# Hybrid decoder layer on one core: the recurrence's outputs and half of its keys transposed by VectorE and scratch memory

## The chip, the cores and the metric

The kernel runs on one core of a Trainium2 chip. The metric is the device time of one execution in microseconds.

## What is computed

One layer of a decoder with two branches. A prompt of 2048 rows of 1024 numbers is normalised and modulated (h) and projected by one weight. Branch A is sliding-window attention over 128 rows with sinks. Branch B is a gated linear recurrence with four heads of 128: with decay f, keys k, queries q and values i, each head carries a 128x128 state over the rows. Both branches are gated with a SiLU, projected, merged by sigmoid gates and projected back.

```
o, s_new = hgrn2_chunked(q, log_f, k_in, i, s0)
yb = rms_norm(o, o_norm_g) * silu(zb)
g_a, g_b = split(sigmoid(h @ w_merge + b_merge))
y = g_a * (ya @ w_proj_a) + g_b * (yb @ w_proj_b)
out = x + gate * (y @ w_out)
```

Beside the prompt, eight sample rows go through the same layer with their own caches and states. Everything is fp32.

## The kernel before, in words

The prompt is worked off in 4 blocks (`it`) of 512 rows, each of 4 tiles of 128. A block is a list of 68 dense units (`UNITS`, line 36): 4 "B" and 4 "A" (attention's projections), 4 each of "za", "f", "qb", "ib", "zb" (units 8 to 27), then from unit 28 the merges: "ga" and "gb" (sigmoid gates, units 28 to 35 are 0 to 3 of both), "pa" and "pb" (the branches' projections, from unit 36 and 37 on), and from unit 60 the output. A dense unit is 24 matmuls with a moving tile of 512 ("pa" and "pb": 12), since every operand is split into a high and a low part of a reduced format and three products are added. Units alternate between the PSUM banks D0 and D1.

Everything else of TensorE is a side task, hung behind one half of a dense unit: `at_half(it, n, ...)` puts a task behind half n, so half 70 is the first half of unit 35 and half 71 the second. All engines walk through the same list of units and halves in order, each doing its part of a task; the numbers in the list are the whole schedule. In a second half the order is fixed: ScalarE first evacuates the unit (`evac`; for a gate it waits for the unit's end), then makes the high parts of the weight blocks attached to it (`split_hi`), and then the side tasks; GpSimd first makes the low parts of those weight blocks (`split_lo`, four subtractions), then the side tasks.

The recurrence in a block, with all of it transposed so that the head's 128 features lie on the partitions:

- seven levels (halves 42 to 54) build the decayed `qq`, `kk` and the score matrix `AT`;
- for tile t at unit 28 + t: "KT" turns the keys of the tile, [features, rows] to [rows, features], with four TensorE transposes into bank XC, and ScalarE copies them to `kst` (lines 936 and 1125); in the second half "o" makes the output rows (into XB; ScalarE copies it into `kk` in place of the keys and squares it into `acc` for the norm), and "st" makes the state update with `kst` as weights (into XA; VectorE adds it to `state`);
- "onorm" (unit 32): VectorE computes the four tiles' root mean squares and scales the outputs in `kk`;
- "yT" (halves 67 to 70, a tile each): TensorE turns the scaled outputs back to [features, rows] with four transposes, VectorE multiplies them with the gate `szb` into a slot of `yf`, ScalarE makes the high part `yb_hi` (`high`), GpSimd the low part `yb_lo` (`low`, line 1713).

The first "pb" (unit 37, half 74) waits until all four low parts are there: `s.wait_ge("yl", 16 * it + 8)` (line 735).

SyncE issues all DMAs from one queue, in order. A weight block of 512 KB (`w_raw`, a ring of three) is loaded when the block three before it has been split (`weights`, line 528). Other transfers are events in the same queue, placed by unit (`later`, line 539). In blocks 0 and 1 "bursts" on TensorE (line 797) multiply the raw weight blocks with the sample's rows, and wait for their loads.

Of the kernel before, what the change touches and what calls it, by code (L numbers as in the profile page):

```python
# [15 lines left out]
TB, NIT = 512, 4  # L16
P, KT, NT = 128, D // 128, TB // 128
# [114 lines left out]

AHEAD = {0: (), 1: (5, 7), 2: (1, 3, 5, 7), 3: (1, 3, 5, 7)}
# [23 lines left out]
for it in range(NIT):  # L157
# [38 lines left out]
    for _t in range(NT):  # L196
        put(it, 28 + _t, 0, "KT", _t, "XC")
        put(it, 28 + _t, 1, "o", _t, "XB")
        put(it, 28 + _t, 1, "st", _t, "XA")
    put(it, 32, 0, "onorm", 0)  # L200
    for _t in range(NT):
        at_half(it, 67 + _t, "yT", _t, "XB" if _t % 2 else "XA")
# [47 lines left out]
for _it in range(NIT):  # L250
    for _u in UNITS:
        if _u in TH:
# [6 lines left out]
           "lvl", "dgp", "at0", "smax", "p_exp", "p_norm", "kst", "on", "yf", "yh", "yl", "y7f", "y7h", "y7l", "x_in0", "x_in1", "xst", "rstd",  # L259
# [63 lines left out]
def build(nc, A, O):  # L323

    ctx = ExitStack()
    with ctx:
# [53 lines left out]
        acc = sb("acc_t", [P, TB])  # L380
        kst = sb("kst_t", [P, HB, P])
# [11 lines left out]
        AT32 = kst[:, :, :].rearrange("p h (t i) -> p (h t) i", t=NT)  # L393
# [12 lines left out]
        first.close()  # L406
        yb_hi, yb_lo = sb("yb_hi_t", [P, 4, TB], F32R), sb("yb_lo_t", [P, 4, TB], F32R)
# [6 lines left out]
        szb = qT  # L414
        y_hi, y_lo = sb("y_hi_t", [P, KT, TB], F32R), sb("y_lo_t", [P, KT, TB], F32R)
# [87 lines left out]
        def _(sp):  # L503
# [36 lines left out]
            for it in range(NIT):  # L540
# [6 lines left out]
                later.setdefault(b0 + 5, []).append(("vr", it, 0))  # L547
                later.setdefault(b0 + 59, []).append(("xr", it, 0))
# [14 lines left out]
            def event(what, it, a):  # L563
                if what == "xst":
# [108 lines left out]
        def _(pe):  # L673
# [88 lines left out]
            def side(it, task, a, key):  # L762
# [209 lines left out]
        def _(act):  # L972
# [99 lines left out]
            def side(it, task, a, key):  # L1072
# [52 lines left out]
                elif task == "KT":  # L1125
                    s.full(*key)
                    if it or a:
                        s.full(*((it, "st", a - 1) if a else (it - 1, "st", 3)))
                    s.free(fn(kst[:, :, :], bank[:, :].rearrange("p (h n) -> p h n", h=HB), ACT.Copy), *key)
                elif task == "o":  # L1130
                    s.full(*key)
                    if it or a:
                        s.freed(*((it, "o", a - 1) if a else (it - 1, "o", 3)))
                    fn(kk[:, :, P * a:P * a + P], bank[:, 0:512].rearrange("p (h n) -> p h n", h=HB), ACT.Copy)
                    for h in range(HB):
                        ins = fn(acc[:, P * h:P * h + P], bank[:, P * h:P * h + P], ACT.Square,
# [9 lines left out]
            for it in range(NIT):  # L1146
                for u in range(NU):
                    for hf_ in (0, 1):
# [9 lines left out]
                        for task, a, _, key in SIDE.get((it, u, hf_), []):  # L1158
# [10 lines left out]
                            if task == "yT":  # L1169
                                s.freed(it, "yT", a)  # L1170
# [8 lines left out]
        def _(dve):  # L1179
# [244 lines left out]
            def side(it, task, a, key):  # L1424
# [117 lines left out]
                elif task == "st":  # L1542
# [4 lines left out]
                    free(ins, *key)  # L1547
                elif task == "onorm":
                    s.freed(it, "o", 3)
                    do(ts(oss, oss, 1.0 / P, EPS, ALU.mult, ALU.add))  # L1550
                    rsqrt(orst, oss, ow1, ow2)
                    for t in range(NT):
                        o = kk[:, :, P * t:P * t + P]
                        s.done(tt(o, o, orst[:, HB * t:HB * t + HB].unsqueeze(2).broadcast_to([P, HB, P]), ALU.mult), "on")
# [294 lines left out]
```

## Time and profile before

| what | us |
|---|---|
| median of three runs (1558.32 to 1558.43) | 1558.33 |
| span of the profiled execution | 1555.9 |
| TensorE busy | 1527.1 |
| GpSimd busy | 826.0 |
| VectorE busy | 787.0 |
| ScalarE busy | 540.7 |

For the profiled execution the span, from its first to its last instruction, is what is listed; its own device time is not listed beside it. The page gives busy times, the span in slices, and the chain of work that ended last, followed back from the last instruction to what released it at each step. TensorE's rows are pipelined: one row's duration is longer than the distance to the next, so distances between starts tell what a stretch costs. The mean granted clock over the span is 0.996.

### The profile page before, as it was taken

To read this page: it belongs to the slowest core of one execution; us is meant where nothing else is said; L and a number is where in the kernel's file an instruction comes from. 1 tells how busy PE (TensorE), PEld (TensorE's weight loads), DVE (VectorE), ACT (ScalarE), POOL (GpSimd) and SP (SyncE) were. 2 spreads that over 40 slices of the span, in tenths; PEclk is the share of its full clock that TensorE was granted. 3 is DMA by queue.
4 is the path that set the end of the run, shared out by engine and by line. 5 is a ranking of instruction groups with operands and counts; after the bars stand their busy time and mean duration, and the time that the engine had idled before them with its cause. 6 is when DMAs were issued, how large, how long until landed. Compare 5 with 4: busy or idle time off the path is not lost.

```text
span 1555.9 us, 31655 instructions
## 1 busy us (share of the span) xinstructions
PE 1527.1 (98%) x13048; PEld 1243.0 (80%) x13048; DVE 787.0 (51%) x1900; ACT 540.7 (35%) x1119; POOL 826.0 (53%) x1074
## 2 busy tenths in 40 slices
PE   5999999999999999999999999999999999999998
PEld 2777788877888788888779878888888978888886
DVE  4767464234558866232544774622453775623132
ACT  4334324334322532434331452243432353143330
POOL 0525434557863643365773472437786363437671
PEclk9999999999999999999999999999999999999999
DMA  9612211334453321233343231223544231222351
GB/s 339 243 55 83 83 57 55 111 133 158 168 197 108 110 70 57 82 109 108 137 164 135 92 120 43 83 66 114 208 154 149 75 110 56 78 72 91 102 167 60
DMA packets 62790, 178.94 MB, mean 115 GB/s; under 512 B 7086, under 2 KB 18695, under 8 KB 61864
## 3 DMA queue, kind: packets, MB, share of 16 engines
q1 hardware_dynamic: 62648, 176.93, 33.4%
q8 instruction: 103, 1.69, 0.5%
q14 instruction: 39, 0.32, 0.1%
HBM read 162.84 MB, written 11.96 MB: 112 GB/s over the span
## 4 chain that ended last, share of the span: by engine, by line
PE 95%; DVE 3%; DMA 1%; SPq 1%; issue 1%; ACT 0%; DVEq 0%
PE ps_D L758 56%; PE ps_D L755 25%; PE ps_XCD L820 2%; PE ps_XB L896 1%; PE ps_XB L949 1%; PE ps_XA L954 1%; PE ps_XA L921 1%; PE ps_XA L932 1%; PE ps_XB L948 1%; PE ps_XA L896 1%; DMA th_t<-in_w_ada 1%; SPq L507 1%; PE ps_XB L932 0%; PE ps_XCD L831 0%; PE ps_XCD L939 0%
## 5 line engine op out<-in xcount | busy, mean ns | idle before, releaser
L1702 POOL TENSOR_TENSOR w_lo_t<-w_raw,w_hi_t 128x256 fp32r<-128x256 f32 x920 | 681.0, 775 | 599.7 <-ACT w_hi_t L980 599.4
L758 PE MATMUL ps_D<-h_hi_t,w_hi_t 128*128 128x512 f32 x1024 | 411.2, 402 | 0.0
L758 PE MATMUL ps_D<-h_hi_t,w_lo_t 128*128 128x512 f32 x1024 | 399.6, 390 | 0.0
L758 PE MATMUL ps_D<-h_lo_t,w_hi_t 128*128 128x512 f32 x1024 | 399.5, 390 | 0.0
L980 ACT ACTIVATE w_hi_t<-w_raw 128x1024 fp32r<-128x1024 f32 x232 | 240.0, 1051 | 124.6 <-PE ps_D L755 61.6
L758 PEld LDWEIGHTS ps_D<-h_hi_t,w_hi_t 128*128 128x128 f32 x1024 | 192.3, 188 | 46.3 <-issue 8.9
L758 PEld LDWEIGHTS ps_D<-h_hi_t,w_lo_t 128*128 128x128 f32 x1024 | 192.2, 188 | 41.8
L758 PEld LDWEIGHTS ps_D<-h_lo_t,w_hi_t 128*128 128x128 f32 x1024 | 192.6, 188 | 36.5
L755 PE MATMUL ps_D<-w_hi_t,h_hi_t 128*128 128x384 f32 (+1 forms) x384 | 141.6, 369 | 1.0 <-DVE yf_t L1342 1.0
L755 PE MATMUL ps_D<-w_lo_t,h_hi_t 128*128 128x384 f32 (+1 forms) x384 | 136.6, 356 | 0.0
L755 PE MATMUL ps_D<-w_hi_t,h_lo_t 128*128 128x384 f32 (+1 forms) x384 | 136.3, 355 | 0.0
L755 PE MATMUL ps_D<-w_hi_t,y_hi_t 128*128 128x512 f32 x256 | 100.2, 391 | 1.5 <-issue 1.5
L755 PE MATMUL ps_D<-w_hi_t,y_lo_t 128*128 128x512 f32 x256 | 99.6, 389 | 0.0
L755 PE MATMUL ps_D<-w_lo_t,y_hi_t 128*128 128x512 f32 x256 | 99.6, 389 | 0.0
L1376 DVE SCALAR_TENSOR_TENSOR acc_t<-th_t,ps_D 128x512 f32<-128x512 f32 x24 | 16.5, 688 | 130.8 <-PE ps_D L758 130.8
L755 PEld LDWEIGHTS ps_D<-w_hi_t,h_hi_t 128*128 128x128 f32 x384 | 72.7, 189 | 11.4 <-issue 4.9
L1047 ACT ACTIVATE th_t<-ps_D,bm_half 128x512 f32<-128x512 f32 x48 | 33.1, 690 | 139.2 <-PE ps_D L758 139.2
L1123 ACT ACTIVATE p_or_hf<-p_or_hf,sm 128x160 f32<-128x160 f32 x128 | 53.3, 419 | 68.5 <-DVE sm L1503 66.6
L755 PEld LDWEIGHTS ps_D<-w_lo_t,h_hi_t 128*128 128x128 f32 x384 | 72.6, 189 | 5.3
L755 PEld LDWEIGHTS ps_D<-w_hi_t,h_lo_t 128*128 128x128 f32 x384 | 72.8, 190 | 4.7
L1394 DVE TENSOR_TENSOR acc_t<-ps_D,gate_bc 128x512 f32<-128x512 f32 x32 | 22.1, 692 | 107.1 <-PE ps_D L755 107.0
L1456 DVE TENSOR_TENSOR qq<-qq,ff 128x1024 f32<-128x1024 f32 x28 | 40.7, 1452 | 68.6 <-PE ps_XB L896 44.7
(386 smaller groups left out, 2332.9 us busy)
## 6 DMA issues: line engine op xcount, KB each, us to landing
w_raw<-in_w_blocks SPq DMA_DIRECT2D x232, 512.0 KB, 3.4
xr<-in_x_prompt SPq DMA_DIRECT2D x16, 512.0 KB, 5.0
x_or_AT<-in_x_prompt SPq DMA_DIRECT2D x14, 512.0 KB, 4.8
out_dram<-xr SPq DMA_DIRECT2D x12, 512.0 KB, 2.8
x_or_AT<-in_x_turned SPq DMA_DIRECT2D x3, 1024.0 KB, 5.6
p_or_hf<-in_x_turned SPq DMA_DIRECT2D x3, 1024.0 KB, 6.2
out_dram<-xr SPq DMA_DIRECT2D x8, 256.0 KB, 2.0
ibtok<-vtok SPq DMA_DIRECT2D x8, 192.0 KB, 3.5
```

The lines of the kernel that those rows point to most:

```text
L507: s.done(sp.dma_start(dst, src, **kw), name, by=16)
L755: ins = mm(bank[:, 0:P * nb].rearrange("p (n c) -> p n c", c=P), a[:, k, P * j:P * j + P], w[:, s0:s0 + nb, k, :], start=go, stop=end)
L758: ins = mm(bank[:, :], w[:, s0, k0 + k, :], a[:, k, :], start=go, stop=end)
L820: ins = mm(dst, hS[:, k, :], raw[:, :, k, :], start=k < 4, stop=k >= 4)
L896: ins = mm(bank[row:row + left, m * col:m * col + m], kk[:, h, c + 32 * g:c + 32 * g + left], right, start=True, stop=True)
L980: s.done(fn(w_hi[:, SLOT[n % NB]], w_raw[:, n % NRAW], ACT.Copy), "w_hi")
L1047: s.leave(fn(dst, bank[:, :], ACT.Tanh, scale=0.5, bias=bm_half[:, c:c + 1]), it, u)
L1123: fn(p_t[:, m, :], p_t[:, m, :], ACT.Exp, bias=negm[:, m:m + 1], accum_out=rsum[:, m:m + 1])
L1376: leave(stt(acc[:, :], thx("ga", j), 1.0, bank[:, :], ALU.add, ALU.mult), it, u)
L1394: leave(tt(acc[:, 0:w], bank[:, 0:w], gate_bc[:, c0:c0 + w], ALU.mult), it, u)
L1456: s.done(tt(qr, qr, fl[:, :, :, 0:1].broadcast_to(shape), ALU.mult))
L1702: ins = g_.tensor_tensor(w_lo[:, c, k:k + 2], w_raw[:, n % NRAW, k:k + 2], f32(w_hi[:, c, k:k + 2]), ALU.subtract)
```

## The change

Two kinds of TensorE turns are replaced: all of "yT" (16 turns in all), and "KT" for tiles 2 and 3 (8 turns). In their place VectorE transposes a half of `kk` (two tiles, 4 x 256 columns) in place, in blocks of 32x32; SyncE stores the half to scratch memory (`zk`, `zo`, 512 KB), waits until it has landed, and loads it back with four DMAs whose pieces are runs of 32 numbers, so that the blocks come to stand where a full transpose has them. Each half has its own store and loads: "ks" and "kl" for the keys, "os" and "ol" for the two halves of the output.

- The keys' half (`kD`, half 56) lands in `k_turned`, and "st" 2 and 3 read it as weights there. ScalarE's "o" 2 waits for the keys' store before it overwrites them.
- The norm is done in two halves (halves 60 and 64), each ending with the transpose (`oD`).
- "yD" (halves 65, 66, 69, 70) is VectorE's multiplication with the gate, out of the loaded half; "yT" (halves 66, 67, 70, 71) is now only the high part on ScalarE and the low part on GpSimd.
- The loaded outputs lie over `acc` and `kst`, and over `qq`; ScalarE's squares go to a slot of `yf` instead of `acc`.

```diff
+KEYS_TURNED = (1,)
+O_AT, ON_AT, YD_AT, YT_AT = (57, 59, 61, 63), (60, 64), (65, 66, 69, 70), (66, 67, 70, 71)
+KS_AT, KL_AT, OS_AT, OL_AT = (28, 28), (28, 28), (30, 32), (31, 32)
...
     for _t in range(NT):
-        put(it, 28 + _t, 0, "KT", _t, "XC")
-        put(it, 28 + _t, 1, "o", _t, "XB")
-        put(it, 28 + _t, 1, "st", _t, "XA")
-    put(it, 32, 0, "onorm", 0)
+        if _t // 2 not in KEYS_TURNED:
+            put(it, 28 + _t, 0, "KT", _t, "XC")
+        at_half(it, O_AT[_t], "o", _t, "XB")
+        at_half(it, O_AT[_t], "st", _t, "XA")
+    for _r in KEYS_TURNED:
+        at_half(it, 56, "kD", _r)
+    for _r in range(2):
+        at_half(it, ON_AT[_r], "onorm", _r)
     for _t in range(NT):
-        at_half(it, 67 + _t, "yT", _t, "XB" if _t % 2 else "XA")
+        at_half(it, YD_AT[_t], "yD", _t)
+        at_half(it, YT_AT[_t], "yT", _t)
...
+                if what == "ks":
+                    s.wait_ge("kD", len(KEYS_TURNED) * it + KEYS_TURNED.index(a) + 1)
+                    s.wait_ge(f"kt_in{a}", 64 * it)
+                    load(zk[a].rearrange("i q (h t) j p -> (i q) h (t j p)", t=2), kk[:, :, half], f"kz{a}")
+                elif what == "kl":
+                    s.wait_ge(f"kz{a}", 16 * (it + 1))
+                    for j in range(4):
+                        load(k_turned[32 * j:32 * j + 32, a].rearrange("p h t (i c) -> p (h t) i c", c=32),
+                             zk[a, :, :, :, j].rearrange("i q n p -> q n i p"), f"kt_in{a}")
+                elif what == "os":
+                    s.wait_ge("oD", 2 * it + a + 1)
+                    s.wait_ge(f"ot_in{a}", 64 * it)
+                    load(zo[a].rearrange("i q (h t) j p -> (i q) h (t j p)", t=2), kk[:, :, half], f"oz{a}")
+                elif what == "ol":
+                    s.wait_ge(f"oz{a}", 16 * (it + 1))
+                    s.full(it, "o" if a else "st", 3 if a else 1)
+                    for j in range(4):
+                        load(o_turned[a][32 * j:32 * j + 32].rearrange("p h t (i c) -> p (h t) i c", c=32),
+                             zo[a, :, :, :, j].rearrange("i q n p -> q n i p"), f"ot_in{a}")
...
                 elif task == "st":
-                    s.freed(it, "KT", a)
+                    if a < 2:
+                        s.freed(it, "KT", a)
+                    else:
+                        s.wait_ge("kt_in1", 64 * (it + 1))
                     for h in range(HB):
-                        ins = mm(bank[:, P * h:P * h + P], kst[:, h, :], ibtok[:, a, P * h:P * h + P],
+                        left = kst[:, h, :] if a < 2 else k_turned[:, 1, h, a % 2, :]
+                        ins = mm(bank[:, P * h:P * h + P], left, ibtok[:, a, P * h:P * h + P],
                                  start=True, stop=True)
-                elif task == "yT":
-                    s.wait_ge("on", 4 * it + a + 1)
-                    for h in range(HB):
-                        ins = tr(bank[:, P * h:P * h + P], kk[:, h, P * a:P * a + P], ident[:, :])
...
+                elif task == "kD":
+                    half = kk[:, :, 256 * a:256 * a + 256]
+                    do(v.transpose(half, half), "kD")
                 elif task == "onorm":
-                    s.freed(it, "o", 3)
-                    do(ts(oss, oss, 1.0 / P, EPS, ALU.mult, ALU.add))
-                    rsqrt(orst, oss, ow1, ow2)
-                    for t in range(NT):
+                    s.freed(it, "o", 2 * a + 1)
+                    c, half = slice(8 * a, 8 * a + 8), kk[:, :, 256 * a:256 * a + 256]
+                    do(ts(oss[:, c], oss[:, c], 1.0 / P, EPS, ALU.mult, ALU.add))
+                    rsqrt(orst[:, c], oss[:, c], ow1[:, c], ow2[:, c])
+                    for t in (2 * a, 2 * a + 1):
...
+                    s.settle()
+                    do(v.transpose(half, half), "oD")
-                elif task == "yT":
-                    s.full(*key)
-                    free(stt(yf_slot(16 * it + 4 + a), bank[:, 0:512].rearrange("p (h n) -> p h n", h=HB), og_half[:, 0:1],
-                             szb[:, :, P * a:P * a + P], ALU.mult, ALU.mult), *key)
+                elif task == "yD":
+                    s.wait_ge(f"ot_in{a // 2}", 64 * (it + 1))
+                    do(stt(yf_slot(16 * it + 4 + a), o_turned[a // 2][:, :, a % 2], og_half[:, 0:1],
+                           szb[:, :, P * a:P * a + P], ALU.mult, ALU.mult), "yt")
```

GpSimd's list in block 0, from the recurrence to the merges, before: `yb_lo_t` is the low part of y, `w_lo_t<-w_raw` the splits of weight blocks (four rows a block).

```order
L1702 TENSOR_TENSOR w_lo_t<-w_raw,w_hi_t 128x256 x52
L1718 TENSOR_TENSOR yb_lo_t<-yf_t,yb_hi_t 128x4x128 x2
L1702 TENSOR_TENSOR w_lo_t<-w_raw,w_hi_t 128x256 x4
L1718 TENSOR_TENSOR yb_lo_t<-yf_t,yb_hi_t 128x4x128 x2
L1702 TENSOR_TENSOR w_lo_t<-w_raw,w_hi_t 128x256 x8
```

And now:

```order
L1753 TENSOR_TENSOR w_lo_t<-w_raw,w_hi_t 128x256 x48
L1769 TENSOR_TENSOR yb_lo_t<-yf_t,yb_hi_t 128x4x128
L1753 TENSOR_TENSOR w_lo_t<-w_raw,w_hi_t 128x256 x4
L1769 TENSOR_TENSOR yb_lo_t<-yf_t,yb_hi_t 128x4x128
L1753 TENSOR_TENSOR w_lo_t<-w_raw,w_hi_t 128x256 x4
L1769 TENSOR_TENSOR yb_lo_t<-yf_t,yb_hi_t 128x4x128
L1753 TENSOR_TENSOR w_lo_t<-w_raw,w_hi_t 128x256 x4
L1769 TENSOR_TENSOR yb_lo_t<-yf_t,yb_hi_t 128x4x128
```

The four low parts stood in two pairs, both ahead of the split attached to unit 35. Now they stand singly, a split before each of the last three; the last low part is behind unit 35's split. It is the same in the other blocks.

SyncE's queue in block 0, from the weight loads of the levels to the load of x for the next block's norm, before:

```order
L507 DMA w_raw<-in_w_blocks 128x1024 x26
L507 DMA x_or_AT<-in_x_prompt 128x1024 x2
L507 DMA w_raw<-in_w_blocks 128x1024 x5
```

And now (`z_k`, `z_o` are the scratch memory):

```order
L522 DMA w_raw<-in_w_blocks 128x1024 x22
L522 DMA z_k<-kk 512x1x256
L522 DMA k_turned<-z_k 32x32x32 x4
L522 DMA w_raw<-in_w_blocks 128x1024 x2
L522 DMA z_o<-kk 512x1x256
L522 DMA acc_or_kst<-z_o 32x32x32 x4
L522 DMA w_raw<-in_w_blocks 128x1024 x2
L522 DMA z_o<-kk 512x1x256
L522 DMA qq<-z_o 32x32x32 x4
L522 DMA x_or_AT<-in_x_prompt 128x1024 x2
L522 DMA w_raw<-in_w_blocks 128x1024 x5
```

Three stores with four loads each now stand among the weight loads (in blocks 1 to 3 one weight load stands between the first output store and its loads). Since otherwise loads follow their store at once, the queue waits at each for the store to land.

## Rows read from the trace of the kernel before

**Rows 1.** The page: span, TensorE busy, and the engines on the chain that ended last.

```profile
span 1555.9 us, 31655 instructions
...
PE 1527.1 (98%) x13048; PEld 1243.0 (80%) x13048; DVE 787.0 (51%) x1900; ACT 540.7 (35%) x1119; POOL 826.0 (53%) x1074
...
PE 95%; DVE 3%; DMA 1%; SPq 1%; issue 1%; ACT 0%; DVEq 0%
```

**Rows 2.** Timeline of TensorE, block 2: first matmuls of half 67, "pa" 0, "pb" 0 (start us, us, instruction).

```profile
1045.50 0.39 PE L758 MATMUL ps_D<-h_hi_t,w_hi_t 128*128 128x512 f32 x1
...
1061.09 0.39 PE L758 MATMUL ps_D<-w_hi_t 128*128 128x512 f32 x1
...
1063.81 0.39 PE L758 MATMUL ps_D<-yb_hi_t,w_hi_t 128*128 128x512 f32 x1
```

**Rows 3.** Timeline of TensorE, block 2: first matmuls of both halves of units 30 and 32.

```profile
1019.99 0.48 PE L758 MATMUL ps_D<-h_hi_t,w_hi_t 128*128 128x512 f32 x1
...
1023.16 0.48 PE L758 MATMUL ps_D<-h_hi_t,w_hi_t 128*128 128x512 f32 x1
...
1037.24 0.48 PE L758 MATMUL ps_D<-h_hi_t,w_hi_t 128*128 128x512 f32 x1
...
1040.06 0.39 PE L758 MATMUL ps_D<-h_hi_t,w_hi_t 128*128 128x512 f32 x1
```

**Rows 4.** Timeline of TensorE, block 0: the sample's turn beside unit 30.

```profile
263.62 0.66 PE L831 MATMUL ps_XCD<-ident,srow 128*128 128x128 f32 x4 [0.69 <-ACT kst_t L1129]
```

**Rows 5.** VectorE: a block transpose (ns, min/median/max), and block 2's norm in the timeline.

```profile
L1527 DVE STREAM_TRANSPOSE p_or_hf<-p_or_hf x32: 845/845/848, 110.7 to 1299.2; 128x640 f32<-128x640 f32 x32
...
1037.59 1.12 DVE L1545 SCALAR_TENSOR_TENSOR state<-state,ff,ps_XA 128x128 f32<-128x128 f32 x4 [7.50 <-PE ps_XA L954]
1038.75 0.65 DVE L1550 TENSOR_SCALAR sm<-sm 128x16 f32<-128x16 f32 x1
...
1042.36 2.50 DVE L1554 TENSOR_TENSOR kk<-kk,sm 128x512 f32<-128x512 f32 x4
```

**Rows 6.** The DMA view of 452 to 461 us, and a DMA issue of the page.

```profile
DMA packets 4377, 2.84 MB, mean 315 GB/s; under 512 B 140, under 2 KB 4195, under 8 KB 4375
...
out_dram<-xr SPq DMA_DIRECT2D x12, 512.0 KB, 2.8
```

**Rows 7.** Timeline of ScalarE, block 2, around the start of "pa" 0.

```profile
1059.34 0.63 ACT L1069 ACTIVATE yb_hi_t<-yf_t 128x512 fp32r<-128x512 f32 x1 [2.34 <-DVE yf_t L1557]
1061.29 0.69 ACT L1047 ACTIVATE th_t<-ps_D,bm_half 128x512 f32<-128x512 f32 x1 [1.31 <-PE ps_D L758]
1061.87 2.00 ACT L980 ACTIVATE w_hi_t<-w_raw 128x1024 fp32r<-128x1024 f32 x2
```

**Rows 8.** Timeline of GpSimd, block 2, the same stretch.

```profile
1056.57 2.82 POOL L1702 TENSOR_TENSOR w_lo_t<-w_raw,w_hi_t 128x256 fp32r<-128x256 f32 x4 [1.12 <-ACT w_hi_t L980]
1059.36 2.54 POOL L1718 TENSOR_TENSOR yb_lo_t<-yf_t,yb_hi_t 128x512 fp32r<-128x512 f32 x2
1063.00 6.06 POOL L1702 TENSOR_TENSOR w_lo_t<-w_raw,w_hi_t 128x256 fp32r<-128x256 f32 x8 [1.11 <-ACT w_hi_t L980]
```

**Rows 9.** Timeline of TensorE, block 1: first matmuls of "pa" 0 and "pb" 0.

```profile
687.88 0.39 PE L758 MATMUL ps_D<-w_hi_t 128*128 128x512 f32 x1
...
691.79 0.40 PE L758 MATMUL ps_D<-yb_hi_t,w_hi_t 128*128 128x512 f32 x1
```

**Rows 10.** Timeline of VectorE, block 0: the state update of tile 3.

```profile
279.59 1.12 DVE L1545 SCALAR_TENSOR_TENSOR state<-state,ff,ps_XA 128x128 f32<-128x128 f32 x4 [8.65 <-PE ps_XA L954]
```

**Rows 11.** Timeline of SyncE's queue, block 0: three weight loads, the first at 288.77.

```profile
288.77 8.13 SPq L507 DMA_DIRECT2D w_raw<-in_w_blocks  x3
```

**Rows 12.** Windows before unit 0: us, busy us of each engine (instructions), PEclk, DMA share, GB/s.

```profile
28.50:32.00 3.50, 3.50 (x18) 0.85 (x12) 3.02 (x10) 0.97 (x2) 1.03 (x1) 0.53 1.06 414
35.00:38.50 3.50, 1.95 (x16) 1.86 (x16) 3.47 (x6) 2.48 (x4) 0.73 (x3) 1.00 0.65 220
38.50:45.50 7.00, 5.34 (x20) 5.34 (x21) 6.29 (x19) 2.33 (x4) 5.90 (x7) 0.51 1.00 408
```

More of the change, by code:

```diff
@@ L379, in build @@
         qa, q3 = (yf[:, :, c:c + w].rearrange("p s (n d) -> p s n d", d=DH) for c, w in ((0, 384), (384, 128)))
-        acc = sb("acc_t", [P, TB])
-        kst = sb("kst_t", [P, HB, P])
+        acc_kst = sb("acc_or_kst", [P, 2 * TB])
+        acc, kst = acc_kst[:, 0:TB], acc_kst[:, TB:].rearrange("p (h n) -> p h n", h=HB)
         hS, yS = sb("hS_or_yS", [P, KT, 32]), sb("cT_or_ab", [P, KT, 32])
@@ L392, in build @@
         ps_s = kst[0:8]
-        AT32 = kst[:, :, :].rearrange("p h (t i) -> p (h t) i", t=NT)
+        AT32 = kst.rearrange("p h (t i) -> p (h t) i", t=NT)
         sq_in = ibS[:, 0:256]
@@ L406, in build @@
         first.close()
+        k_turned = first.enter_context(nc.sbuf_tensor("k_turned", [P, 2, HB, 2, P], F32))
+        first.close()
+        first = ExitStack()
         yb_hi, yb_lo = sb("yb_hi_t", [P, 4, TB], F32R), sb("yb_lo_t", [P, 4, TB], F32R)
@@ L414, in build @@
         szb = qT
+        o_turned = [t.rearrange("p (h t n) -> p h t n", h=HB, t=2)
+                    for t in (acc_kst[:, :], qq.rearrange("p h n -> p (h n)")[:, 0:1024])]
+        zk, zo = (nc.dram_tensor(f"z_{n}", [2, 4, 32, 2 * HB, 4, 32], F32).ap() for n in "ko")
         y_hi, y_lo = sb("y_hi_t", [P, KT, TB], F32R), sb("y_lo_t", [P, KT, TB], F32R)
@@ L547, in _ @@
                 later.setdefault(b0 + 5, []).append(("vr", it, 0))
+                for r in range(2):
+                    if r in KEYS_TURNED:
+                        later.setdefault(b0 + KS_AT[r], []).append(("ks", it, r))
+                        later.setdefault(b0 + KL_AT[r], []).append(("kl", it, r))
+                    later.setdefault(b0 + OS_AT[r], []).append(("os", it, r))
+                    later.setdefault(b0 + OL_AT[r], []).append(("ol", it, r))
                 later.setdefault(b0 + 59, []).append(("xr", it, 0))
@@ L563, in event @@
             def event(what, it, a):
-                if what == "xst":
+                half = slice(256 * a, 256 * a + 256)
+                if what == "ks":
[17 more added lines that the diff above has]
+                             zo[a, :, :, :, j].rearrange("i q n p -> q n i p"), f"ot_in{a}")
+                elif what == "xst":
                     s.full(it, "o", 3)
@@ L1126, in side @@
                     s.full(*key)
-                    if it or a:
-                        s.full(*((it, "st", a - 1) if a else (it - 1, "st", 3)))
-                    s.free(fn(kst[:, :, :], bank[:, :].rearrange("p (h n) -> p h n", h=HB), ACT.Copy), *key)
+                    if a:
+                        s.full(it, "st", a - 1)
+                    s.free(fn(kst, bank[:, :].rearrange("p (h n) -> p h n", h=HB), ACT.Copy), *key)
                 elif task == "o":
@@ L1133, in side @@
                         s.freed(*((it, "o", a - 1) if a else (it - 1, "o", 3)))
+                    if a // 2 in KEYS_TURNED:
+                        s.wait_ge(f"kz{a // 2}", 16 * (it + 1))
+                    s.wait_ge("yl", 16 * it + 4)
                     fn(kk[:, :, P * a:P * a + P], bank[:, 0:512].rearrange("p (h n) -> p h n", h=HB), ACT.Copy)
                     for h in range(HB):
-                        ins = fn(acc[:, P * h:P * h + P], bank[:, P * h:P * h + P], ACT.Square,
+                        ins = fn(yf[:, 1, P * h:P * h + P], bank[:, P * h:P * h + P], ACT.Square,
                                  accum_out=oss[:, HB * a + h:HB * a + h + 1])
@@ L1169, in _ @@
                             if task == "yT":
-                                s.freed(it, "yT", a)
+                                s.full(it, "st", 3)
+                                s.wait_ge("yt", 4 * it + a + 1)
                                 high(yb_hi[:, :, P * a:P * a + P], 16 * it + 4 + a)
```

4 lines of the change are left out of this document (2 added, 2 removed).

## Prediction

> **What bounds the kernel now.** I read the page first [rows 1]: TensorE is busy for 1527.1 of 1555.9 us and has 95% of the chain that ended last. So a microsecond that another engine saves is worth nothing unless TensorE waits for it, one taken from TensorE's list is worth itself, and one that TensorE has to wait comes on top. The sum is made on this span, 1555.9 us. The median of the three runs, 1558.3 us, is 2.4 us longer; I carry this difference over unchanged. About 0.2% (3.1 us) is what a measurement of this kernel can tell from no change.
>
> The second view is TensorE's timeline around the turns. A half unit of the dense work takes 2.72 us when nothing stands in it (the first matmul of "pa" 0 to that of "pb" 0) [rows 2]. From half 67 to "pa" 0 there are five halves with four turns of y in them: 1061.09 - 1045.50 = 15.59 us where five bare halves are 13.60 [rows 2]. A turn of y (four transposes, and the dense matmuls refilling behind them) therefore costs 0.50 us, though its four records add up to 1.1. A turn of the keys costs what unit 30's first half has over unit 32's, which also follows "o" and "st" but holds nothing: 3.17 against 2.82 us, plus some 0.13 us of refilling in the next half: 0.48 us [rows 3].
>
> **What comes off TensorE.** 16 turns of y at 0.50 are 8.0 us, and 8 turns of the keys (tiles 2 and 3 of each block) at 0.48 are 3.8 us. One stall goes as well: in block 0 the sample's turn at unit 30 waited 0.69 us for ScalarE's copy of the turned keys out of the bank that both use [rows 4]; that copy is gone. **Sum: 12.5 us less**, some 3 us of it in each block, and all of it on the path.
>
> **What is added and hidden.** VectorE gets three block transposes of 1024 elements a block, and the 14 small steps of the norm twice instead of once. A transpose of 640 elements takes 0.845 us, so one of 1024 is about 1.35 us; the norm's small steps run from 1038.75 to 1042.36, 3.6 us [rows 5]. That is some 8 us a block on an engine that is 51% busy, beside dense work on TensorE. I cost it at nothing by itself; it matters where a transfer starts behind it.
>
> No row of before has pieces of 128 bytes in bulk. The nearest is the load of the sample states: in 9 us the engines moved 4195 packets under 2 KB, almost all of 512 bytes, at 315 GB/s [rows 6]. 4096 pieces of 512 bytes (2.1 MB) at that rate take 6.7 us. A set of four loads has 4096 pieces of 128 bytes: by bytes alone 1.7 us, by pieces 6.7 us, and twice that, 13.3 us, if a short piece costs double. I take 6.7 us, because the count of pieces is the same, and add 1.5 us for issue and landing. The store moves 512 KB like the stores of the output, 2.8 us to landing [rows 6].
>
> The keys have slack: turned at the start of unit 28, they are wanted at the end of unit 30, three units on. With SyncE coming to the store some 6 us late (it first waits for a split of weights), store and loads end about 17 us after the start of unit 28; "st" 2 is due after some 25 us.
>
> The second half of the output has less. In block 2 VectorE ends "st" 3 at 1038.7, now 1.0 us earlier; norm 3.6, two scalings 1.25 (half of the 2.50), the transpose 1.35, store 2.8, loads 8.2: it lands at about 1055.0. "pa" 0 will start at 1061.1 - 3.0 = 1058.1. So yD 2 and 3 are done in time for what follows, with some 2 us to spare.
>
> **What is added and not hidden** is the place of the last piece of y. It was handed over at half 70 and is now at half 71, and at a second half ScalarE and GpSimd do other things first. ScalarE takes the gate of unit 35 out of the bank, which it can't before that unit ends, then copies the high part of a weight block, and only then the high part of y; GpSimd splits that weight block before it makes the low part. The trace has this chain without the y: with "pa" 0 starting at 1061.09, ScalarE's gate starts at 1061.29, the weight copy at 1061.87 [rows 7], GpSimd's split at 1063.00 [rows 8]. A split is 2.82 us, the low part of a y tile half of 2.54, so the low part of tile 3 is ready 1.91 + 2.82 + 1.27 = 6.0 us after "pa" 0 starts. "pb" 0, whose first matmul waits for all of it, would start after 2.7 us [rows 2]. **TensorE stalls 3.3 us** in a block like 2 or 3. In block 1 a burst stands in the way and "pb" 0 starts 3.9 us after "pa" 0 [rows 9]: 2.1 us. These stalls don't depend on how fast the transfers are.
>
> In block 0 two more things are late. There VectorE has "st" 3 done at 280.7 [rows 10], 1.7 us earlier now; by the same steps the loads are issued at about 288 and done at 296. Only then come the two x tiles and the weight block that SyncE issued at 288.77 before [rows 11]; 1.5 MB at 315 GB/s is 5 us, so that block lands at 301. ScalarE wants it at about 297 and holds its queue, the y tiles among it. Worked through, the low part of tile 3 comes 2.9 us later than above: 6.2 us. If the pieces go at the byte rate this part is zero, and both ends are kept.
>
> Stalls: 6.2 + 2.1 + 3.3 + 3.3 = 14.9 us. The clock adds something. Before unit 0, after a stretch with only 16 matmuls of nine columns in 3.5 us, the granted clock fell from 1.00 (2.4 GHz) to about 0.5 (1.2 GHz): 0.53 over 3.5 us once, 0.51 over 7 us once [rows 12]. Dense work that runs 3.5 us at half rate loses 1.7 us. A stall of 3.3 us is shorter than what came before those falls, one of 6.2 is not: from none to four falls, and I take two, 3.4 us. By the Trainium skill, page TensorE: Matmul & The Clock Gate (Rules for kernel authors), gaps between matmul bursts put the array back on the lower clock; if that held for all four stalls, the sum would be 3.4 us longer than mine.
>
> **The sum:** 1555.9 - 12.5 + 14.9 + 3.4 = 1561.7 us of span, 5.8 us more, or a time of **1564.1 us**, 0.4% slower.
>
> **Rival 1: the short pieces are slow.** If a 128-byte piece costs twice a 512-byte one, a set takes 6.7 us longer. In blocks 2 and 3 it then lands 4.7 us after yD 2 is wanted, in block 1 about 4, in block 0 the full 6.7 counts, and four falls of the clock are likely: 14.9 + 20 + 6.8 - 12.5 = 29 us more, 1587 us. For it: each piece is a quarter of the nearest one's size, and the reads jump. Against it: 6.7 us already pays as much for a piece as for one four times as long. The Trainium skill speaks against this change here: DMA: Bandwidth & Descriptors (Rules for kernel authors) puts a plain DMA with a rearranged access pattern at 19 times the hardware's own transpose, and its Specifications say that transfers under 512 bytes run below line rate. No row shows such a factor; the pieces here are whole runs of 32 numbers. Nineteen times 1.7 us would be a set of 32 us, 19 us more in each block than this rival and some 1660 us: chance 0.02 of this rival's 0.18.
>
> **Rival 2: stalls and savings cancel.** The stall at "pb" 0 stays, but block 0 has no more than the others and the clock never falls: 3.3 x 3 + 2.1 = 12.0 against 12.5 us, 1557.8 us. This is the other side, not slower: it decides where stalls and clock together stay under 15.6 us, that is at 3.9 us a block. For it: nothing in the trace says that a stall of 3.3 us is enough for a fall, and by bytes the loads are quick. Chance 0.23.
>
> **Rival 3: faster.** If the handover of tile 3 is not what ends last, because "pb" 0's matmuls already issued hide part of the wait or the turns cost TensorE nearer 0.65 us than 0.50, the time goes down: halved stalls with no fall of the clock are 6 - 12.5, 1551.8 us. Rows 7 and 8 leave little room for this, since every step of the chain stands there with its start. Chance 0.07.
>
> **Rival 4: SyncE's queue.** SyncE now sits on the store until it has landed, and the weight loads are behind it. In blocks 0 and 1 bursts on TensorE wait for raw weights directly; in block 0 the weight block for the burst at unit 33 lands, by my steps, about a microsecond before it is wanted. If it misses, 1 to 5 us more, 1567 us. It is inside the range, at 0.10.
>
> **Chances.** Forecast 0.42, rival 1 0.18, rival 2 0.23, rival 3 0.07, rival 4 0.10. Slower by over 0.2% is the forecast, rivals 1 and 4: 0.70. Within 0.2% is rival 2: 0.23; faster 0.07. The range runs from 1557 (rival 2 with its uncertainty) to 1582 (short pieces at about 1.7 times); left out are rival 3 and the upper part of rival 1. The likeliest case has 1561 to 1570 for itself, since block 0 and the clock can each go by 3 us.
>
> **What would show it.** In the profile after: no matmuls of the y turns, and half of the key turns; a wait of TensorE for GpSimd's low part of y, four times, the first matmul of "pb" 0 behind it, 3.3 us in blocks 2 and 3 and less in block 1; dense halves at 2.72 us between them; a granted clock under 1 after some of these waits. The loads of the turned output landing some 7 to 9 us after issue show the middle price; 3 us or 14 us show its ends. The forecast is wrong if TensorE's waits at "pb" 0 sum to under 9 us, or if it waits at "st" 2 or for VectorE, which I cost at nothing.

## The result, and the profile after

| | median us | lowest to highest | against before (95%) |
|---|---|---|---|
| before, same chip | 1558.32 | 1558.03 to 1558.43 | |
| with the change | 1564.40 | 1563.17 to 1566.84 | 1.0044 (1.0030 to 1.0058) |

The change costs 6.1 us, 0.4%; 1564.1 was predicted. The profiled execution is the slowest of those after: its own time is 1566.84, its span 1564.7, 8.8 us over the span before. The page, against [rows 1]:

```profile
span 1564.7 us, 31594 instructions
...
PE 1521.3 (97%) x12952; PEld 1236.9 (79%) x12952; DVE 813.1 (52%) x1972; ACT 535.5 (34%) x1111; POOL 829.1 (53%) x1074
...
DMA packets 119048, 191.52 MB, mean 122 GB/s; under 512 B 57199, under 2 KB 74952, under 8 KB 118121
...
q8 instruction: 102, 1.67, 0.5%
...
PE 91%; DVE 4%; SPq 1%; POOL 1%; ACT 1%; issue 1%; DMA 1%; DVEq 0%
```

TensorE has 96 matmuls less and is busy 5.8 us less, and yet the span is longer: its share of the chain fell from 95 to 91%, and VectorE, GpSimd and ScalarE took most of the rest. What they hold up stands in the list of TensorE's waits (us in total, times, longest); the two of its rows that name another engine and that before did not have:

```profile
PE ps_D L799 <- POOL yb_lo_t L1769: 11.6, 4, 3.2
...
PE ps_XB L989 <- ACT yf_t L1180: 1.3, 1, 1.3
```

TensorE's timeline has the four waits, each in front of the first matmul of "pb" 0, blocks 0 to 3:

```profile
308.20 0.77 PE L799 MATMUL ps_D<-yb_hi_t,w_hi_t 128*128 128x512 f32 x1 [3.19 <-POOL yb_lo_t L1769]
...
697.42 0.48 PE L799 MATMUL ps_D<-yb_hi_t,w_hi_t 128*128 128x512 f32 x1 [2.01 <-POOL yb_lo_t L1769]
...
1068.73 0.76 PE L799 MATMUL ps_D<-yb_hi_t,w_hi_t 128*128 128x512 f32 x1 [3.19 <-POOL yb_lo_t L1769]
...
1429.34 0.47 PE L799 MATMUL ps_D<-yb_hi_t,w_hi_t 128*128 128x512 f32 x1 [3.19 <-POOL yb_lo_t L1769]
```

In block 2, where the turns of y stood in [rows 2], TensorE now runs from half 67 to "pa" 0 without a gap:

```profile
1049.06 0.39 PE L799 MATMUL ps_D<-h_hi_t,w_hi_t 128*128 128x512 f32 x1
...
1062.66 0.39 PE L799 MATMUL ps_D<-w_hi_t 128*128 128x512 f32 x1
```

The five halves take 13.60 us, as bare as they can be, where it was 15.59. And this is the chain behind the wait, ScalarE's and GpSimd's timelines against [rows 7, 8]:

```profile
1062.86 0.69 ACT L1088 ACTIVATE th_t<-ps_D,bm_half 128x512 f32<-128x512 f32 x1 [3.29 <-PE ps_D L799]
1063.44 1.05 ACT L1021 ACTIVATE w_hi_t<-w_raw 128x1024 fp32r<-128x1024 f32 x1
1064.39 0.62 ACT L1110 ACTIVATE yb_hi_t<-yf_t 128x512 fp32r<-128x512 f32 x1
```

```profile
1064.57 2.79 POOL L1753 TENSOR_TENSOR w_lo_t<-w_raw,w_hi_t 128x256 fp32r<-128x256 f32 x4 [1.37 <-ACT w_hi_t L1021]
1067.32 1.26 POOL L1769 TENSOR_TENSOR yb_lo_t<-yf_t,yb_hi_t 128x512 fp32r<-128x512 f32 x1
```

"pa" 0 starts at 1062.66; the low part of the last tile is ready at 1068.58, 5.9 us later (6.0 predicted), and "pb" 0 starts at 1068.73.

To book all of it I compared the starts of the dense halves in the two traces. ("issue" is time in which TensorE waited for nothing that the profile shows.) After minus before, us:

| what | block 0 | 1 | 2 | 3 | sum | predicted |
|---|---|---|---|---|---|---|
| units 28 to 35 without their turns | -3.6 | -2.8 | -3.0 | -3.0 | -12.4 | -12.5 |
| stall at "pb" 0 | 3.4 | 2.2 | 3.4 | 3.4 | 12.2 | 14.9 |
| lower clock in the four halves from "pb" 0 on | 2.9 | 0.1 | 1.6 | 1.8 | 6.4 | 3.4 |
| unit 31, wait for ScalarE | 1.6 | | | | 1.6 | 0 |
| units 19 and 23, "issue" | | 3.0 | | 0.5 | 3.5 | 0 |
| rest (start of the kernel, units 24 and 59) | -0.9 | -0.8 | -0.4 | -0.4 | -2.5 | 0 |
| | | | | | 8.8 | 5.8 |

Two rows of it need a look. The clock, in windows behind the four waits (us, busy of each engine, PEclk, DMA share, GB/s):

```profile
307.70:315.00 7.30, 6.79 (x18) 5.45 (x19) 1.09 (x2) 0.00 (x0) 3.11 (x5) 0.55 0.20 72
697.00:704.00 7.00, 6.58 (x29) 5.50 (x30) 2.07 (x3) 1.58 (x2) 4.27 (x6) 1.00 0.45 150
1068.70:1071.50 2.80, 2.77 (x7) 2.22 (x8) 0.00 (x0) 0.00 (x0) 2.63 (x4) 0.50 0.44 171
1429.30:1434.00 4.70, 4.66 (x14) 3.73 (x15) 0.00 (x0) 0.00 (x0) 2.65 (x4) 0.64 0.48 146
```

After the three waits of 3.19 us the granted clock is at or near 0.5 (1.2 GHz) for some microseconds, after the one of 2.01 us it stays at 1.00. And the stops in block 1 that no engine is named for, in TensorE's timeline at units 19 and 23 (a group of small matmuls, cut by a pause):

```profile
574.38 0.95 PE L919 MATMUL ps_XCD<-qq,kk 128*32 128x32 f32 x85
576.89 0.32 PE L919 MATMUL ps_XCD<-qq,kk 128*32 128x32 f32 x11 [1.55 <-issue]
...
604.76 0.30 PE L937 MATMUL ps_XB<-qq,kk 128*32 128x16 f32 x12 [0.94 <-issue]
```

Nothing of the change is near there. Before, the 96 matmuls at unit 19 stood in one row.

### The profile page after: what moved, and what is told of

The parts are those of the page before. It is cut to its first block, busy times and chain, and to the rows that moved or that the text cites. A ratio compares the mean times of both kernels' runs of the same rounds, so it can differ in the third digit from the quotient of the medians.

```text
span 1564.7 us, 31594 instructions
## 1 busy us (share of the span) xinstructions
PE 1521.3 (97%) x12952; PEld 1236.9 (79%) x12952; DVE 813.1 (52%) x1972; ACT 535.5 (34%) x1111; POOL 829.1 (53%) x1074
## 3 DMA queue, kind: packets, MB, share of 16 engines
q8 instruction: 102, 1.67, 0.5%
## 4 chain that ended last, share of the span: by engine, by line
PE 91%; DVE 4%; SPq 1%; POOL 1%; ACT 1%; issue 1%; DMA 1%; DVEq 0%
PE ps_D L799 54%; PE ps_D L796 25%; PE ps_XCD L861 1%; SPq L522 1%; PE ps_XB L937 1%; PE ps_XA L962 1%; PE ps_XA L973 1%; PE ps_XA L999 1%; PE ps_XB L990 1%; PE ps_XB L989 1%; PE ps_XA L937 1%; POOL w_lo_t L1753 1%; DMA th_t<-in_w_ada 1%; PE ps_XB L973 0%; PE ps_XCD L962 0%
## 5 line engine op out<-in xcount | busy, mean ns | idle before, releaser
L1421 DVE SCALAR_TENSOR_TENSOR acc_or_kst<-th_t,ps_D 128x512 f32<-128x512 f32 x24 | 16.5, 688 | 134.3 <-PE ps_D L799 134.2
L1439 DVE TENSOR_TENSOR acc_or_kst<-ps_D,gate_bc 128x512 f32<-128x512 f32 x32 | 22.1, 692 | 106.0 <-PE ps_D L796 105.9
```

The source lines that it names most:

```text
L1421: leave(stt(acc[:, :], thx("ga", j), 1.0, bank[:, :], ALU.add, ALU.mult), it, u)
L1439: leave(tt(acc[:, 0:w], bank[:, 0:w], gate_bc[:, c0:c0 + w], ALU.mult), it, u)
```

## The experiments

**1. The last tile of y at half 70 again.**

```diff
-YT_AT = (66, 67, 70, 71)
+YT_AT = (66, 67, 70, 70)
```

> The changed kernel with one number changed: the high and low part of the last tile of y are made at half 70, ahead of ScalarE's gate of unit 35 and of GpSimd's split of that unit's weight block, instead of at half 71. Nothing else moves; the transfers, their times and their places stay. Theory A (the place of the last piece of y in ScalarE's and GpSimd's lists is the cause): the low part is ready about 3.5 us earlier, before TensorE gets to the first matmul of pb 0, so the stalls of 3.19, 2.01, 3.19 and 3.19 us go, and with them the three falls of the clock (6.2 us together): 1564.4 less 12.2 less 6.2 = about 1546, and up to 1549 if a microsecond of waiting is left in some blocks. The savings of the turns then show: about 10 us faster than before. Theory B (the transfers are what comes last): the low part comes no earlier, since y 3 itself is there late; the stalls stay near 3 us and the time near 1564. Theory C (the stalls go but the clock's falls have another cause): 1552.

Measured: 1548.36 us (1546.70 to 1549.36), 0.9936 of before (0.9923 to 0.9950), 16.0 us less than with the change as it was. The wait for GpSimd's low part is 0.30 us in block 0 and nothing elsewhere. In block 2 GpSimd makes both low parts ahead of unit 35's split, and "pb" 0 starts at 1058.07 without a wait:

```profile
1055.02 2.54 POOL L1769 TENSOR_TENSOR yb_lo_t<-yf_t,yb_hi_t 128x512 fp32r<-128x512 f32 x2
1057.52 6.05 POOL L1753 TENSOR_TENSOR w_lo_t<-w_raw,w_hi_t 128x256 fp32r<-128x256 f32 x8
```

From the starts of the dense halves: 11.8 us come back at the stalls and 6.1 us at the clock. Theory A holds, and C falls with B: the falls of the clock went together with the stalls. One place in a table was worth more than the whole loss.

**2. The same place in the kernel before**, with no transfer in it.

```diff
-        at_half(it, 67 + _t, "yT", _t, "XB" if _t % 2 else "XA")
+        at_half(it, (67, 68, 69, 71)[_t], "yT", _t, "XB" if _t % 2 else "XA")
```

> The kernel before with one number changed: TensorE's turn of the last tile of y, and with it the gate, the high and the low part of that tile, at half 71 instead of half 70. There is no transpose on VectorE and no transfer through scratch memory in it. Theory A (the place of the last piece is the cause): stalls in front of pb 0 as in the changed kernel or a little longer, since the turn on TensorE and the gate on VectorE now come in that half as well: 12 to 14 us of stalls and 3 to 6 us of lower clock, 1573 to 1578. Theory B (the transfers are the cause): 1558.3, no new wait at pb 0.

Measured: 1571.87 us (1570.14 to 1572.69), 1.0087 of before (1.0073 to 1.0101). The half ahead of "pb" 0 is longer by 2.9, 1.7, 2.9 and 2.9 us, for the same reason:

```profile
PE ps_D L758 <- POOL yb_lo_t L1718: 9.6, 4, 2.7
```

It is 1 us under the range I gave, since these stalls make 10.4 us where theory A had 12 to 14. The clock's part is 4.6 us, inside the 3 to 6: it fell after two of the four waits (1.7 us in block 0, 2.9 in block 3), and not in block 2 after a wait as long as theirs, 2.7 us. The place alone makes stalls of this size, with no transfer in the kernel.

**3. The stall filled with work.** Whether the slow halves behind the stall are due to the stall itself.

```diff
+                        if it > 1:
+                            s.freed(it, "KT", 1)
+                            for n in range(12):
+                                mm(XC[:, :], w_hi[:, s0, n % 4, :], ya_hi[:, n % 4, :], start=True, stop=True)
                         s.wait_ge("yl", 16 * it + 8)
```

> The changed kernel with 12 extra matmuls of 512 columns in blocks 2 and 3, put in front of the wait for the low part of y at pb 0; their results are thrown away, they only keep TensorE at work while it would stand still. Theory A (the stall itself makes the granted clock fall afterwards): the low part still comes when it did, the stall of 3.19 us is filled, no fall of the clock after it, so 1.6 and 1.7 us come back: 3.3 us less than the changed kernel, about 1561. Theory B (the clock falls for another reason, or the lengthened halves after the stall are something else): 0, 1564.4. If the extra matmuls take longer than the stall, some tenths of a microsecond more in each of the two blocks.

Measured: 1562.75 us (1559.56 to 1565.84), 1.0032 of before (1.0021 to 1.0043). Against the 1.0044 of the change the intervals overlap, so the times alone decide nothing. The trace does: the first matmul of "pb" 0 starts at 1070.44 behind the filling, and the windows behind it read

```profile
1070.40:1073.00 2.60, 2.56 (x11) 2.11 (x12) 0.00 (x0) 0.00 (x0) 2.60 (x4) 1.00 0.45 173
1429.80:1434.00 4.20, 4.19 (x18) 3.46 (x19) 0.89 (x2) 0.00 (x0) 2.74 (x4) 1.00 0.37 132
```

where they read 0.50 and 0.64. The halves there are 1.4 and 1.5 us shorter than with the change (3.3 us expected for both), and in block 0, which has no filling, the clock falls as before. So it is TensorE's standing still that the clock answers to, and the price is real.

**4. The sample's row task out of the norm's way.** In block 0 of the change ScalarE stood for 11.89 us behind VectorE, and "o" 3 on TensorE waited for it, as ScalarE's and TensorE's timelines show:

```profile
271.54 0.88 ACT L1140 ACTIVATE smS<-smS,bm_half 128x8 f32<-128x8 f32 x4 [11.89 <-DVE smS L1453]
```

```profile
275.50 0.49 PE L989 MATMUL ps_XB<-state,qq 128*128 128x128 f32 x2 [1.28 <-ACT yf_t L1180]
```

```diff
-        put(0, 30, 0, "srow", 0)
+        put(0, 31, 0, "srow", 0)
```

(on top of experiment 1)

> The kernel of the first experiment with one more number changed: the sample's row task of block 0 (VectorE's adds for it take from 260.1 to 265.5 us in the changed kernel) is put at unit 31 instead of unit 30. Theory A: in block 0 the norm of the first half is no longer behind it, VectorE comes to the sample's column sum earlier, ScalarE no longer stands 11.9 us there, and TensorE's wait of 1.28 us for ScalarE's copy of output tile 2 goes: 1.3 to 1.6 us less than the first experiment. Theory B (the wait comes from the norm or the transpose alone): 0 to 0.3 us less.

Measured: 1547.34 us (1546.49 to 1548.75), 0.9932 of before (0.9920 to 0.9945), 1.0 us under experiment 1, with overlapping intervals, so that the effect rests on the trace. There the half at unit 31 goes from 7.03 to 5.49 us, 1.5 less, and 0.6 is given back at "pb" 0 of block 0, where the wait is now 0.91. The norm in two halves is cheap, but the first half came to stand in front of a task that another engine waited for: the 8 us a block that I had called hidden were not, once.

**5. The keys alone**, on the kernel before: the change's parts for the keys, none of those for the output.

> The kernel before with the first part of the change alone: the keys of tiles 2 and 3 are turned by VectorE and scratch memory, with one store and one set of four loads a block; the outputs are turned by TensorE as before, with the last tile of y at half 70. Theory A (the terms of the sum hold): 8 turns at 0.36 to 0.48 us come off TensorE (2.9 to 3.8 us) and the 0.7 us wait of block 0 for ScalarE's copy of the turned keys goes; no new stall at pb 0: 3.5 to 4.5 us less than before, 1553.5 to 1554.5. Theory B (turns of keys are hidden between the dense matmuls, or the loads take bandwidth or SyncE's queue from the weights): 0 to 1 us less, 1557 to 1558.

Measured: 1552.92 us (1551.37 to 1553.57), 0.9963 of before (0.9950 to 0.9975). The medians differ by 5.5 us, 1.0 more than theory A's range; the spans of the two profiled executions differ by 4.5. By the dense starts it is 4.6 us in this place: 1.0 us a block in units 28 to 31, so 0.49 a turn, and in block 0 the 0.7 us of [rows 4] besides. That is theory A in its cause: no new wait of TensorE stands behind the store and the loads. This part was good from the start.

**6 and 7. TensorE's program shifted.**

```diff
             s.done(ins, "p_T")
+            for n in range(26):
+                tr(XB[:, 9 * (n % 8):9 * (n % 8) + 9], ident[0:9, 0:P], ident[0:9, 0:9])
             s.wait_ge("p_c", 1)
```

(on top of experiment 4; 64 in place of 26 in the other)

> The kernel of the fourth experiment with 26 extra turns of nine columns by TensorE at the very start, where it waits 7.4 us for a load; their results are not used. They do nothing but move every later instruction of TensorE by 26 matmuls and their 26 weight loads in its program. In all four kernels with the change TensorE stops for up to 1.5 us, with nothing that it waits for, behind the same matmul: the 85th of 96 small ones at unit 19 of block 1, and again behind the 116th of 128 small ones at unit 23. Of the kernels without the change one stops there, behind the 59th and for 0.3 us. Theory A (the stop is the loading of TensorE's program, which comes in pieces of fixed size: 103 packets of 16 KB in before for 26096 matmuls and weight loads; where a border falls behind a dense crowd of small matmuls, the next piece is not there yet): the stop at unit 19 moves to about the 59th matmul and shrinks to 0 to 0.4 us, that at unit 23 shrinks or goes: 1.5 to 2.5 us less than the fourth experiment. Theory B (it has to do with data, memory or the throttle): the stops stay behind the 85th and the 116th, and the time stays within 0.5 us.

> As the kernel before in this series, with 64 extra small turns instead of 26. Theory A (program pieces): the border of the piece moves 64 matmuls forward from the 85th, to about the 21st of the 96 at unit 19, and from the 116th to about the 52nd of the 128 at unit 23. A stop behind either of them would be of another length, since other matmuls now fill the piece ahead of it; most of the time from 0 to 1 us at each. Theory B: the stops stay behind the 85th and the 116th with 1.5 and 0.7 us.

Measured with 26: 1545.58 us (1544.58 to 1546.46), 0.9917 of before (0.9903 to 0.9930). The stop at unit 19 is all but gone, and the 96 matmuls stand in one row:

```profile
568.17 1.25 PE L921 MATMUL ps_XCD<-qq,kk 128*32 128x32 f32 x96
```

The half at unit 19 is 1.5 us shorter, that at unit 23 0.9, that at unit 19 of block 3 0.3. The median is 1.8 us under experiment 4, though the intervals of the two against before (0.9903 to 0.9930, 0.9920 to 0.9945) overlap. Measured with 64: 1549.63 us (1547.29 to 1550.30), 0.9940 of before (0.9928 to 0.9953). Both stops of block 1 are gone as well, but there are others where there were none, as in block 2:

```profile
944.22 0.39 PE L801 MATMUL ps_D<-h_hi_t,w_lo_t 128*128 128x512 f32 x1 [0.63 <-issue]
...
977.04 0.37 PE L939 MATMUL ps_XA<-qq,kk 128*32 128x16 f32 x21 [0.45 <-issue]
```

and block 0 has one of 0.48 and a longer stall at "pb" 0 (1.9 us and a fall of the clock; ScalarE stands 2.79 us there for the weight block, 1.74 in experiment 4). So these stops sit at places of TensorE's program and not of its data or its time. In every kernel of the first position (the change and experiments 1, 3, 4, 8 and 10) it stops behind the same 85th matmul; with 26 more it doesn't. With the program of before, 24 matmuls and some waits longer up to there, it stops in experiment 2 alone, behind the 59th, for 0.31 us; in experiment 5, with 8 matmuls fewer than before up to there, behind the 67th, for 0.22 us.

By the page there are 102 packets, 1.67 MB, on the queue called "q8 instruction", against 12952 matmuls and as many weight loads: 254 of them to a packet of 16 KB. The small matmuls go at 11 ns each, so a packet's worth, 127 of them with their weight loads, is used up in 1.4 us there (an estimate from these numbers). The Trainium skill, page Runtime: NRT & Kernel Launch (Instruction fetch mechanics), says the same of the blocks of 16 KiB and 256 instructions, and that the fetch is hidden, since dispatch is slower than filling; here it was hidden in most places, and cost up to 1.6 us in a crowd of small matmuls.

The traces also hold the times of these packets, and they bear it out. In the change one takes from 574.54 to 575.50 us, and TensorE goes on 1.4 us after its end. In the seven other kernels that stop at unit 19 it goes on 1.3 to 1.5 us after the end of such a packet, in the six that stop at unit 23 1.2 to 1.5 us, and behind the two stops shown above 1.35 and 1.38 us. In experiment 6 the packet has ended at 567.48, 0.7 us ahead of the crowd of small matmuls, and 0.2 us of the stop is left. So what TensorE waits for in these stops is its next instructions.

**8. The second half's loads twice.**

```diff
+                    for again in range(a + 1):
+                        if again:
+                            s.wait_ge("ot_in1", 64 * (2 * it + 1))
                         for j in range(4):
```

(on top of experiment 4, with the two waits on this count doubled)

> The kernel of the fourth experiment with the loads of the second half of the output done twice, the second set of four behind the landing of the first. It measures how much slack the transfers have and what a set costs. By the traces so far a set takes some 5.5 us from its first issue to VectorE's first use. Theory A (the transfers have a few microseconds of slack in blocks 1 to 3 and none in block 0): in block 0 the second half and the weight block behind it are 5.5 us later and pb 0 with them, with a fall of the clock of up to 2.9 us; in block 1 the stall stays under 1 us; in blocks 2 and 3 it is 1 to 2.5 us each. In all 8 to 14 us more than the fourth experiment: 1555 to 1561. Theory B (the transfers were all but late everywhere): 5.5 us in each block and four falls of the clock, 1572 to 1577. Theory C (ample slack): under 1 us more.

Measured: 1559.90 us (1558.47 to 1561.47), 1.0010 of before (1.0000 to 1.0019), 12.6 us more. SyncE issues the eight loads of block 2 from 1047.98 on and VectorE starts at 1057.92, 9.9 us later, where a single set took 5.4. TensorE's halves at "pb" 0 are 5.1 us longer in block 0, nothing in block 1, 0.6 in block 2 and 3.3 in block 3, and after the first and the last of these the clock falls again, 1.6 us each. The second set delays the first use by 5.1, 6.1, 4.6 and 5.8 us in the four blocks, so the slack is none in block 0 (where experiment 4 already had its stall of 0.91 us), over 6 us in block 1, some 4 in block 2 and 2.5 in block 3. Theory A, with more slack in the middle than I gave it.

**9. The x tiles behind the weight block**, in block 0, where SyncE's queue had them in front.

```diff
-                    later.setdefault(b0 + 33, []).append(("xst", it, 0))
+                    later.setdefault(b0 + (33 if it else 35), []).append(("xst", it, 0))
```

(on top of experiment 6)

> The kernel of the sixth experiment (26 extra small turns) with one more number changed: in block 0 SyncE issues the loads of two x tiles (1 MB) for the next block at unit 35 instead of 33, so that the weight block which ScalarE wants next is no longer behind them. Theory A (in block 0 the weight block is what comes last: ScalarE waited 1.7 us for it at 298.0 us in the fourth experiment, and TensorE 0.8 to 0.9 us for the low part of y at pb 0): that stall goes, 0.8 to 1 us less, about 1544.7. Theory B (the stall comes from GpSimd's own work, or the x tiles come late for the next block): 0, or some tenths more.

Measured: 1544.90 us (1544.58 to 1545.52), 0.9917 of before (0.9904 to 0.9931). The half ahead of "pb" 0 goes from 2.31 to 1.36 us, bare, as theory A has it; the time is 0.7 under experiment 6, with overlapping intervals. This is the best version: 13 us faster than before, where the change as it was is 6 us slower.

**10. Rows of 4 KB in place of runs of 128 bytes.**

```diff
-                        load(o_turned[a][32 * j:32 * j + 32].rearrange("p h t (i c) -> p (h t) i c", c=32),
-                             zo[a, :, :, :, j].rearrange("i q n p -> q n i p"), f"ot_in{a}")
+                        load(o_turned[a][32 * j:32 * j + 32].rearrange("p h t n -> p (h t n)"),
+                             zo[a, j].rearrange("q n j p -> q (n j p)"), "ot_in1")
```

(for the second half, a = 1, on top of experiment 4)

> The kernel of the fourth experiment with the four loads of the second half of the output reading whole rows of 4 KB instead of runs of 128 bytes: the same bytes, the same number of loads, 128 pieces in place of 4096. The blocks of that half are then not put where a transpose has them, so this half of the output is computed from misplaced numbers. Theory A (the short pieces are what a set costs): the first use by VectorE comes about 2 us sooner behind the first issue than the 5.4 us in block 2 of the fourth experiment, at 3.5 to 4 us, and the transfers behind it in the queue land 2 us sooner, so that the stall of 0.9 us in block 0 goes: 0.9 us less. Theory B (issue and landing are what a set costs, four issues take 2.75 us and a landing 3 us): 5.2 to 5.5 us as before, and no change of the time.

Measured: 1546.79 us (1545.58 to 1549.26), 0.9931 of before (0.9918 to 0.9945). This kernel leaves out the placing of the blocks, so it measures the loads alone. SyncE's and VectorE's timelines of block 2, first of experiment 4 with its short pieces:

```profile
1043.41 2.75 SPq L522 DMA_DIRECT2D qq<-z_o  x4
...
1048.79 1.38 DVE L1608 SCALAR_TENSOR_TENSOR yf_t<-qq,og_half,qT_or_szb 128x512 f32<-128x512 f32 x1 [6.24 <-DMA qq<-z_o]
```

and with whole rows:

```profile
1044.14 1.73 SPq L522 DMA_DIRECT2D qq<-z_o  x4
...
1048.22 0.75 DVE L1612 SCALAR_TENSOR_TENSOR yf_t<-qq,og_half,qT_or_szb 128x512 f32<-128x512 f32 x1 [4.94 <-DMA qq<-z_o]
```

It is 5.4 us against 4.1 from the first issue to the first use in this block. From the first issue to the last landing the short pieces take 0.5 to 1.3 us more in the four blocks, 0.9 us in the mean (5.3 against 4.3), which is no more than what the issue takes longer, 1.0 us a set (0.69 us a load against 0.43). The stall in block 0 goes, 1.0 us. The times don't tell the two kernels apart (1547.34 and 1546.79 us, with overlapping ranges); this profile has one more fall of the clock, behind the stop of 1.60 us at unit 19, that experiment 4 has not. Neither theory had it whole: the pieces cost less than A said, and more than B.

## Why the prediction was right, and where it was not

**The direction and its cause** were right: 12.5 us come off TensorE (12.4 measured), and the last tile's place behind ScalarE's gate and weight copy and GpSimd's split takes as much back in stalls. The chain's 6.0 us were 5.9, the stall of 3.3 us in blocks 2 and 3 was 3.4, that of 2.1 in block 1 was 2.2. Experiments 1 and 2 show from both sides that it is this place: moved back, all but 0.3 us of the stalls goes; moved alone, stalls of 2.7, 1.6, 2.7 and 2.7 us come.

**The term for block 0** was wrong: 6.2 us, measured 3.4. The failing step is the price of a set of four loads, 6.7 us for its pieces and 1.5 us for issue and landing, 8.2 us. From the first issue to the last landing it takes 5.3 to 6.0 us in the trace of the change (in block 0, issued at 288.47, it has landed at 294.46, where I had 296), since I priced a piece of 128 bytes like one of 512. Experiment 10 puts all of a set's short pieces at 0.9 us; what a set costs is four issues and a landing. The late weight block, too, came sooner than the 301 us that I had: ScalarE waited 1.12 us for it, until 298.71, and caught up. This also settles rival 1. The rule of 19 times in the Trainium skill's page DMA: Bandwidth & Descriptors (Rules for kernel authors) compares with the hardware's own transpose, which no run here has; the set of 32 us that I had worked out from it did not come.

**The clock** was undersized for the profiled execution: I took 3.4 us for two falls, and it was 6.4 for three. A fall after a stall of 3.2 us was the rule and not the exception, and the one in block 0 cost 2.9. The Trainium skill's rule on gaps (page TensorE: Matmul & The Clock Gate, section Why this matters for your kernels), which I weighed at 3.4 us more, was nearer to it: three of four, 3.0 us more than my sum.

**Two things I did not have at all**: the wait of 1.6 us for ScalarE at unit 31, because I costed the norm's first half at nothing without asking who stood behind it on VectorE; and 3.5 us of stops in blocks 1 and 3, because I did not think of the program itself as something that is loaded and that 24 matmuls fewer a block shift. With 2.5 us the other way, at the start and at units 24 and 59, the span came out 3.0 us over my sum. The median is nearer than that because the profiled execution is the slowest of the four. The mean clocks of the two fastest (0.996 over 1561.6 us, 0.995 over 1561.0, against 0.993 over 1564.7) say that they had some 9 and 6 us less at 1.2 GHz, an estimate; so 6.4 us for the clock is the high end of what this kernel shows. So 1564.1 hit 1564.4 partly by errors that cancelled: 2.7 us too much of stalls against 3.0 too little of clock.

**Left open**: the pause of 0.6 to 1.7 us at the start of the output units in block 1, which every kernel has, before too, and which a shift of the program doesn't move; it varies by 1 us between kernels. It is of another kind than the stops at units 19 and 23, since no packet of instructions ends in the 9 us before it goes on. Whether 26 is the best shift was not tried.

## What to carry to other kernels

When a hand-over slides by one slot, read what each engine does first in the new slot: here one half unit later meant one gate, one weight copy and one split later, 3.3 us, though the transfers had long landed. Price a stall of TensorE of some 3 us with what the clock takes afterwards, here about half as much again (6.4 us on 12.2). And look for rows that wait on "issue" inside a crowd of small matmuls: if they sit behind the same matmul in every variant, some unused instructions at the start of that engine's program are worth a try.

## What the runs showed of the hardware

- The clock after a stop of TensorE, at "pb" 0: it fell after four of four stops of 3.19 us (three in the change, one in experiment 3), after those of 6.04 and 3.25 in experiment 8, after two of three of 2.7 in experiment 2 and after one of 1.9 in experiment 7; it didn't after two of 2.01 and one of 1.55. At unit 19 it fell after one stop of 1.60 us (experiment 10) and not after five of 1.3 to 1.6. Such a fall costs 1.6 to 2.9 us.
- A load of 128 KB in 1024 pieces of 128 bytes takes 0.69 us to issue from SyncE's queue, in rows of 4 KB 0.43; it lands 3.0 us after issue against 2.6 (medians of experiments 4 and 10).
- VectorE transposes 128x1024 numbers in blocks of 32 in 1.25 us (1.35 estimated).
- TensorE's program comes in packets of 16 KB, one to some 254 matmuls and weight loads. In a crowd of small matmuls TensorE stood still for up to 1.6 us, until 1.2 to 1.5 us after the end of the next packet.
